# A transformer block kernel: weight remainders on GpSimd beside attentions, crossed halves of k in three stages, and another order of ScalarE's work for the queries to the memory

## The chip, the cores and the metric

The kernel runs on one core of one Trainium2 chip. The metric is the device time of one execution in microseconds (us), as the median of several runs. Five engines work side by side, each with its own queue, and wait for each other on semaphores: PE (TensorE, the matrix engine), DVE (VectorE), ACT (ScalarE), POOL (GpSimd) and SP (SyncE, which here only issues DMAs).

## The reference, cut to what matters

256 tokens of width 1024 pass through two layers of a first block (SwiGLU, a mixer, SwiGLU, a per-layer gate `ple`) and then a second block. All is in float32. The parts around the change:

```python
def swiglu(x, w_gate_up, w_down):
    g, u = jnp.split(x @ w_gate_up, 2, axis=-1)
    return (jax.nn.silu(g) * u) @ w_down

def odd_mixer(h, w_in, b_f, w_out):          # layer 1; layer 0 has two attentions (sliding window, and low-rank k and v)
    q, k, v, f_logit = jnp.split(h @ w_in, [w, 2 * w, 3 * w], axis=-1)
    logf = jax.nn.log_sigmoid(f_logit + b_f)
    out = fox_attention(q, k, v, jnp.cumsum(logf, axis=1))
    return out @ w_out

# second block
y_a = moba_attention(q, k, v) @ moba_w_proj
y_b = gmlp_spatial_gating(gu, gv, ...) @ gmlp_w_proj
x = x + (sigmoid(gate_a) * y_a + sigmoid(gate_b) * y_b) @ w_out
x = x + memory_cross_attention(rmsnorm(x, g_xa), rmsnorm(mem, g_mem), w_q, w_kv, w_o)
x = x + peer_ffn(rmsnorm(x, g_ffn), peer_w_q, subkeys, w_down, w_up)
```

## The kernel before, in words

**Weights as a stream.** All large weights are stored as 340 units of 128x2048 float32 (1 MB), four blocks of 128 rows of k by 512 columns. They pass through a ring of three buffers (`RING = 3`), the splitting two units ahead of use (`LEAD = 2`). The units by stage, first unit in brackets: `ffa0` (0), `ev_in` (33), `uq`, `ukv` (39, 40), `ev_out` (41), `ffb0` (45), `ple0` (78), `ffa1` (83), `od_in` (116), `od_out` (128), `ffb1` (132), `ple1` (165), `in2` (170), `moba` (188), `gmlp` (190), `xkv` (192), `out2` (196), `xq` (200), `xo` (202), `peer_q` (204), `peer` (212).

**Each unit, step by step.** SP loads `raw` (`load_unit`, L248); the load of unit u+3 waits until the remainder of unit u is made. ScalarE rounds it to the matrix engine's format, `w_hi` (`split_hi`, L257, one instruction, L262). VectorE makes the remainder `w_lo = raw - w_hi` (`split_lo`, L264, one instruction, L267). PE then multiplies three times into a PSUM bank: `w_hi` by `x_hi` (L300), `w_lo` by `x_hi` (L301), `w_hi` by `x_lo` (L302); a unit is 24 such matmuls of 128x512 where both token tiles use it. `take` (L293) waits for both halves of a unit before the first of them. The activations are split in the same way: ScalarE makes `x_hi` out of PSUM (L327), VectorE `x_lo` (L336), PE transposes them first (L305).

```python
def take(pe, u):
    pe.wait_ge(*act_done["w_hi", u])
    pe.wait_ge(*dve_done["w_lo", u])
    return u % RING
```

**Norms.** ScalarE sums squares (L408), VectorE takes the mean (L413), GpSimd the power -1/2 (`pool_root`, L418). Beside these GpSimd clears a few buffers (L1255 to L1257, L1478, L1832) and issues a few DMAs.

**Attentions.** A chain of steps. In each, PE makes scores (L880), VectorE the maxima (L962, L1000) and the inverse of the sums, ScalarE the exponentials (L938), VectorE scales them, two halves at a time, both operand and result in SBUF (L987, in the queries to the memory L1010), PE transposes (L305) and multiplies with the values (L907). Between the steps PE works on products of the weight units at hand, and each engine's list has the splits of the next units put in by hand.

**Order.** Every engine's program is written out by hand, in the order in which the functions `tensor_...`, `scalar_...`, `vector_...`, `pool_...` and `sync_...` call things; there is no scheduler. In a stage's first block of 512 columns the units come as k 0 to 3, then k 4 to 7 of the same block, and the second needs the second four chunks of `x_hi` and `x_lo`. In `od_in` the forget gate's small work stands between units: PE transposes its logits `zt` after unit 2, and uses their logarithm in the matmuls of L1329 after unit 3; in between VectorE and ScalarE compute it (ScalarE with two table loads, L1386 and L1388). In `scalar_cross` (L1928) the order is: squares, wait for the power (in `scalar_normed`, L428), `w_hi` of unit 202, the table load for Exp (L1933), the scaled queries (L816, `scale_out`), `w_hi` of unit 203. PE needs these queries for its transposes (L305).

Of the kernel before, what the change touches and what calls it, by code (L numbers as in the profile page):

```python
# [15 lines left out]
P = 128  # L16
# [20 lines left out]
RING = 3  # L37
# [103 lines left out]
def build(nc, a, stop=None):  # L141
    with ExitStack() as ctx:
# [121 lines left out]
        def split_lo(e, u):  # L264
            if u < N_UNITS and u not in plain:
                e.wait_ge(*act_done["w_hi", u])
                e.tensor_tensor(w_lo[:, u % RING, :, :], raw[:, u % RING, :, :], f32(w_hi[:, u % RING, :, :]),  # L267
                                ALU.subtract).then_inc(*dve_done.mark("w_lo", u))
# [24 lines left out]
        def take(pe, u):  # L293
            pe.wait_ge(*act_done["w_hi", u])
            pe.wait_ge(*dve_done["w_lo", u])
            return u % RING
# [131 lines left out]
        def scalar_normed(act, key, part, name, prev, banks=(6, 7, 2, 3)):  # L428
            for i in (0, 1):
                scalar_lift(act, key, 4 * part + 2 * i, KC, banks[2 * part + i], lambda k: gain(name, k), x_hi)  # L430
            if part:
                wait_h(act, prev, 1)
                scalar_squares(act, key, h_tile, D, 0)
                act.wait_ge(*pool_done["rstd", key])
# [8 lines left out]


# [103 lines left out]
        def tensor_up(pe, key, c, u, between=None, ready=None, meanwhile=None, free=None):  # L548
            for i in range(2):
                s = u + i if u + i < 2 else take(pe, u + i)  # L550
                for t in range(NT):
                    if i == 0 and free:
                        free(t)
                    if i == 0 and t == 1 and between:
                        between()
                    for k in range(UB):
                        kk = i * UB + k
                        if ready and t == 0:
                            ready(kk)
                        last = product(pe, bank[gu(c)[t]][:, :], s, k, BLK, x_hi[:, kk, t * P:(t + 1) * P],  # L560
                                       x_lo[:, kk, t * P:(t + 1) * P], kk == 0, kk == KC - 1)
                    last.then_inc(*pe_done.mark("unit", u + i, t))
                    if i == 1:
                        pe_done.also("up", key, c, t)
                pe_done.also("used", u + i)
                if i == 0 and meanwhile:
                    meanwhile()
# [25 lines left out]
        def tensor_ffn(pe, n, prev, hand):  # L593
# [3 lines left out]
            tensor_up(pe, n, 0, ffn_up(n, 0), lambda: tensor_normed(pe, n, prev, 1), ready)  # L597
            for c in range(1, NFC):
                def free(t, c=c):
                    pe.wait_ge(*dve_done["mid", n, 0 if c == 2 else c - 1, t])  # L600
                tensor_up(pe, n, c, ffn_up(n, c), free=free if c > 1 else None, meanwhile=lambda c=c: tensor_back(pe, n, c - 1))
                if c >= 2:
                    take_down(pe, n, c - 2)
                    for half in range(2):
                        tensor_down_half(pe, n, c - 2, half)
                    pe_done.also("used", ffn_down(n, c - 2))
# [11 lines left out]
        def scalar_ffn(act, n, prev, hand):  # L618
# [17 lines left out]
            split_hi(act, ffn_up(n, 0) + 1 + LEAD)  # L636
            silu(0)
            for c in range(1, NFC):
                split_hi(act, ffn_up(n, c) + LEAD)
                split_hi(act, ffn_up(n, c) + 1 + LEAD)  # L640
# [9 lines left out]
        def vector_ffn(dve, n, prev, hand):  # L650
# [21 lines left out]
            split_lo(dve, ffn_up(n, 0) + 1 + LEAD)  # L672
            both(0)
            for c in range(1, NFC):
                split_lo(dve, ffn_up(n, c) + LEAD)
                split_lo(dve, ffn_up(n, c) + 1 + LEAD)
# [2049 lines left out]
```

## Time and profile before

| | |
|---|---|
| runs | 2117.62 us median of 3 (2116.42 to 2120.5) |
| profiled execution, its own time | 2120.12 us |
| its span | 2118.3 us |
| granted TensorE clock, mean over it | 0.997 |
| PE busy | 99% of the span, 10466 matmuls |
| VectorE, ScalarE, GpSimd busy | 63%, 50%, 1% |
| one `w_hi` on ScalarE, one `w_lo` on VectorE | 1915 ns, 2290 ns, 336 of each |
| chain that ended last | 94% on PE |

The span runs from the first to the last instruction of the profiled execution, and its own time has 1.8 us more around it. In a timeline row the first number is the start in us from the span's beginning, the second the duration; a group of consecutive instructions of one kind has one row, with their count behind an x. The bracket at the end says how long the engine was idle before it, and what it had waited for. PEclk is the granted clock of TensorE, 1.00 for 2.4 GHz and 0.50 for 1.2 GHz.

### The profile page before, as it was taken

Reading aid. Unit: us, or ns where it says so; the run is one execution under the profiler, and the core shown is the slowest. Engines: PE = TensorE matmul, PEld = TensorE weight load, DVE = VectorE, ACT = ScalarE, POOL = GpSimd, SP = SyncE. Lnnn points to the kernel's source line nnn. Section 1 sums busy time; section 2 is a strip of 40 time slices with the busy share of each in tenths; the row PEclk is TensorE's granted clock in tenths of the full one; section 3 lists DMA queues with packets and bytes.
Section 4 is the critical chain, followed back from the end, with each engine's and each line's share of the span. In section 5 each row is a group of like instructions: output and inputs, shape, how many; then the busy total and the mean of one; then the engine's idle time right before and its main releaser. Section 6 shows DMA issues by size and latency. Waiting matters only on the chain.

```text
span 2118.3 us, 25812 instructions
## 1 busy us (share of the span) xinstructions
PE 2091.8 (99%) x10466; PEld 1744.0 (82%) x10466; DVE 1338.4 (63%) x1793; ACT 1049.0 (50%) x1262; POOL 31.2 (1%) x42
## 2 busy tenths in 40 slices
PE   9999899999999999999999999999999999999998
PEld 7888788888888888888888878888888888888887
DVE  5445765456545566554675756799888656666665
ACT  5445564446444556444657555546455544444443
POOL 0100000000000000000100000000000000000000
PEclk9999999999999999999999999999999999999999
DMA  6654335554555442555554535577799997676772
GB/s 254 215 183 177 119 133 192 196 180 180 182 196 180 177 140 105 194 183 192 186 185 160 177 119 199 179 243 238 240 270 272 281 329 310 261 268 258 268 258 109
DMA packets 96596, 433.72 MB, mean 205 GB/s; under 512 B 7680, under 2 KB 41104, under 8 KB 51936
## 3 DMA queue, kind: packets, MB, share of 16 engines
q1 hardware_dynamic: 95152, 426.50, 57.2%
q0 software_dynamic: 1328, 5.58, 0.8%
q8 instruction: 84, 1.38, 0.2%
q14 instruction: 32, 0.26, 0.0%
HBM read 397.45 MB, written 34.60 MB: 204 GB/s over the span
## 4 chain that ended last, share of the span: by engine, by line
PE 94%; DVE 3%; ACT 1%; issue 1%; DMA 0%; POOL 0%; SPq 0%; POOLq 0%; DVEq 0%
PE bank L300 28%; PE bank L302 28%; PE bank L301 28%; PE bank L305 5%; PE bank L2224 2%; DVE w_lo L267 1%; PE bank L907 1%; PE bank L880 1%; PE bank L2057 0%; DMA h<-in_x 0%; DVE x_lo L336 0%; DVE arena L800 0%; ACT w_hi L262 0%; ACT arena L938 0%; ACT x_hi L327 0%
## 5 line engine op out<-in xcount | busy, mean ns | idle before, releaser
L267 DVE TENSOR_TENSOR w_lo<-raw,w_hi 128x2048 fp32r<-128x2048 f32 x336 | 768.7, 2290 | 510.0 <-ACT w_hi L262 509.9
L262 ACT ACTIVATE w_hi<-raw 128x2048 fp32r<-128x2048 f32 x336 | 643.0, 1915 | 721.2 <-PE bank L302 704.7
L300 PE MATMUL bank<-w_hi,x_hi 128*128 128x512 f32 (+1 forms) x2080 | 822.0, 395 | 4.6 <-DVE x_lo L336 3.3
L302 PE MATMUL bank<-w_hi,x_lo 128*128 128x512 f32 (+1 forms) x2080 | 810.1, 389 | 0.0
L301 PE MATMUL bank<-w_lo,x_hi 128*128 128x512 f32 (+1 forms) x2080 | 809.4, 389 | 0.0
L300 PEld LDWEIGHTS bank<-w_hi,x_hi 128*128 128x128 f32 x2080 | 391.5, 188 | 84.0 <-ACT gated L408 3.1
L302 PEld LDWEIGHTS bank<-w_hi,x_lo 128*128 128x128 f32 x2080 | 391.0, 188 | 82.1
L301 PEld LDWEIGHTS bank<-w_lo,x_hi 128*128 128x128 f32 x2080 | 391.7, 188 | 76.2
L300 PE MATMUL bank<-w_hi,a_hi 128*128 128x512 f32 x624 | 246.6, 395 | 0.2 <-DVE a_lo L995 0.2
L302 PE MATMUL bank<-w_hi,a_lo 128*128 128x512 f32 x624 | 243.2, 390 | 0.0
L301 PE MATMUL bank<-w_lo,a_hi 128*128 128x512 f32 x624 | 243.0, 389 | 0.0
L302 PEld LDWEIGHTS bank<-w_hi,a_lo 128*128 128x128 f32 x624 | 117.1, 188 | 24.6
L300 PEld LDWEIGHTS bank<-w_hi,a_hi 128*128 128x128 f32 x624 | 117.3, 188 | 23.2 <-DVE a_lo L995 0.4
L301 PEld LDWEIGHTS bank<-w_lo,a_hi 128*128 128x128 f32 x624 | 117.3, 188 | 22.9
L622 ACT ACTIVATE gated<-bank,small 128x256 f32<-128x256 f32 x88 | 41.8, 475 | 119.6 <-PE bank L302 119.4
L2308 DVE TENSOR_TENSOR gated<-bank,arena 128x512 f32<-128x512 f32 x64 | 65.2, 1060 | 53.7 <-PE bank L305 53.7
L305 PE MATMUL bank<-consts_sb,arena 128*128 128x128 f32 (+2 forms) x566 | 78.8, 277 | 9.4 <-DVE arena L987 4.9
L305 PEld LDWEIGHTS bank<-consts_sb,arena 128*128 128x128 f32 (+2 forms) x566 | 66.5, 139 | 21.2 <-issue 4.5
L656 DVE SCALAR_TENSOR_TENSOR mid<-bank,small,gated 128x256 f32<-128x256 f32 x88 | 41.9, 479 | 44.8 <-ACT gated L622 44.8
L327 ACT ACTIVATE x_hi<-bank,gains_sb 128x256 fp32r<-128x256 f32 x92 | 36.1, 476 | 57.6 <-PE bank L305 57.6
L2214 DVE TENSOR_TENSOR arena<-arena 128x1024 bf16<-128x1024 bf16 x96 | 60.4, 683 | 0.0
L336 DVE SCALAR_TENSOR_TENSOR x_lo<-bank,gains_sb,x_hi 128x256 fp32r<-128x256 f32 x92 | 38.1, 477 | 20.7 <-ACT x_hi L327 20.5
(202 smaller groups left out, 1222.8 us busy)
## 6 DMA issues: line engine op xcount, KB each, us to landing
raw<-in_w SPq DMA_DIRECT2D x338, 1024.0 KB, 4.8
parked_t<-arena SPq DMA_DIRECT2D x32, 512.0 KB, 8.9
arena<-parked_t SPq DMA_DIRECT2D x8, 2048.0 KB, 9.4
arena<-parked_a SPq DMA_DIRECT2D x32, 512.0 KB, 5.8
parked_a<-one_i SPq DMA_DIRECT2D x21, 512.0 KB, 7.3
parked_a<-mid SPq DMA_DIRECT2D x11, 512.0 KB, 7.0
raw<-in_w SPq DMA_DIRECT2D x8, 256.0 KB, 6.3
one_i<-in_alibi POOLq DMA_DIRECT2D x1, 1024.0 KB, 5.2
```

Of the source, the lines that this page charges most:

```text
L262: act.activation(w_hi[:, u % RING, :, :], raw[:, u % RING, :, :], ACT.Copy).then_inc(*act_done.mark("w_hi", u))
L267: e.tensor_tensor(w_lo[:, u % RING, :, :], raw[:, u % RING, :, :], f32(w_hi[:, u % RING, :, :]), ALU.subtract).then_inc(*dve_done.mark("w_ ...
L300: pe.matmul(out, hi, w_hi[:, s, b, 0:width], start=start, stop=False)
L301: pe.matmul(out, hi, w_lo[:, s, b, 0:width], start=False, stop=False)
L302: return pe.matmul(out, lo, w_hi[:, s, b, 0:width], start=False, stop=stop)
L305: return pe.transpose(out, src, ident[0:src.shape[0], 0:src.shape[0]])
L336: dve.scalar_tensor_tensor(lo[:, k, :], part, gain_of(k), f32(hi[:, k, :]), ALU.mult, ALU.subtract).then_inc(*dve_done.mark("lift_lo", key ...
L622: act.activation(gated[:, 2 * (c % 2) + t, :], bank[gu(c)[t]][:, 0:FC], ACT.Silu, scale=rstd(t)).then_inc(*act_done.mark("silu", n, c, t))
L656: dve.scalar_tensor_tensor(mid[:, t, c % 2 * FC:(c % 2 + 1) * FC], bank[gu(c)[t]][:, FC:2 * FC], rstd(t), gated[:, 2 * (c % 2) + t, :], AL ...
L2214: last = dve.tensor_tensor(hot_j[:, slot, 1 + k, :, :, :], hot_j[:, slot, 0, :, :, :], token_cols(2 + k), ALU.mult)
L2224: last = pe.matmul(bank[banks[j // 4]][:, j % 4 * P:(j % 4 + 1) * P], hot_i[:, slot, j // 2, :, j % 2], hot_j[:, slot, 1 + k, j // 2, :, j ...
L2308: dve.tensor_tensor(gated[:, 2 * b:2 * b + 2, :], bank[back_banks(c)[b]][:, :].rearrange("p (f t) -> p f t", f=2), tables[:, piece % N_TAB ...
```

## The change

Three parts.

- **Remainders on GpSimd.** For the units in `lent` GpSimd makes `w_lo` instead of VectorE: units 41, 42, 43 (`ev_out`), 128, 129, 130 (`od_out`), 188, 189 (`moba`), 190, 191 (`gmlp`), 200, 201 (`xq`), 202, 203 (`xo`), 204, 205 (`peer_q`). The list holds sixteen units, and the built program has sixteen such instructions on GpSimd. The loads and PE wait for GpSimd's semaphore at those units. GpSimd's list is put in order around its powers and DMAs, and the load of `p` for `ple` moves ahead of the power of `ffb`.
- **Crossed halves.** In `ffa1`, `od_in` and `in2` the second and the third unit change places in the stored weights and in PE's order: k 0 to 3 of block 0, k 0 to 3 of block 1, k 4 to 7 of block 0, k 4 to 7 of block 1. The first block is therefore finished one unit later. In `od_in` the forget gate's logits keep their place in PE's list by count of units. Some splits move ahead of the work on block 0's result.
- **ScalarE's order in `scalar_cross`.** The Exp table load moves between the squares and the wait for the power, and `w_hi` of unit 202 moves behind the scaled queries.

```diff
+        CROSSED = ("ffa1", "od_in", "in2")
+        for n in CROSSED:
+            u = first[n]
+            stored[u + 1], stored[u + 2] = u + 2, u + 1
...
+        lent = {first[n] + i for n, units in (("ev_out", (0, 1, 2)), ("od_out", (0, 1, 2)), ("moba", (0, 1)), ("gmlp", (0, 1)),
+                                              ("xq", (0, 1)), ("xo", (0, 1)), ("peer_q", (0, 1))) for i in units}
+
+        def remainder_made(u):
+            return (pool_done if u in lent else dve_done)["w_lo", u]
...
-                sp.wait_ge(*dve_done["w_lo", u - RING])
+                sp.wait_ge(*remainder_made(u - RING))
...
+        def remainders(pool, u0, u1):
+
+            for u in range(u0, u1):
+                if u in lent:
+                    pool.wait_ge(*act_done["w_hi", u])
+                    pool.tensor_tensor(w_lo[:, u % RING, :, :], raw[:, u % RING, :, :], f32(w_hi[:, u % RING, :, :]),
+                                       ALU.subtract).then_inc(*pool_done.mark("w_lo", u))
...
+            tensor_up_half(pe, n, 0, 0, first[n], lambda: tensor_normed(pe, n, prev, 1), ready)
+            if n in CROSSED:
+                tensor_up_half(pe, n, 1, 0, first[n] + 1)
+                tensor_up_half(pe, n, 0, 1, first[n] + 2, None, ready)
+                tensor_up_half(pe, n, 1, 1, first[n] + 3)
+                tensor_back(pe, n, 0)
...
             unit(0)
+            unit(2)
             unit(1)
             pe.wait_ge(*act_done["f_hi"])
...
-            unit(2)
+            unit(3)
             pe.wait_ge(*dve_done["forget", "zt"])
...
-            unit(3)
+            unit(4)
             pe.wait_ge(*dve_done["forget", "logf"])
...
-            unit(4)
             unit(5)
...
-            for i in range(8):
+            for i in (0, 2, 1, 3, 4, 5, 6, 7):
                 unit(i)
...
-            scalar_normed(act, "xa", 1, "xa", prev, XA_BANKS)
-            split_hi(act, q0 + LEAD)
-
-            act.activation(small[:, 80:81], gains[:, 0:1], ACT.Exp, scale=0.0)
+
+            scalar_normed(act, "xa", 1, "xa", prev, XA_BANKS,
+                          lambda: act.activation(small[:, 80:81], gains[:, 0:1], ACT.Exp, scale=0.0))
             act.wait_ge(*pe_done["block", "xq", 0, 0])
             scale_out(act, 0, bank[4][:, :], qn_x[:, 0, :]).then_inc(*act_done.mark("xq"))
+            split_hi(act, q0 + LEAD)
             split_hi(act, q0 + 1 + LEAD)
```

**ScalarE, the queries to the memory.** Before (x_hi is the lift of the second token tile, gated holds the squares, L816 is the scaled queries, L938 the exponentials):

```order
L327 ACTIVATE x_hi<-bank,gains_sb 128x256 x4
L408 ACTIVATE gated,small<-h 128x1024 x2
L262 ACTIVATE w_hi<-raw 128x2048
L1933 ACT_TABLE_LOAD
L1933 ACTIVATE small<-gains_sb 128x1
L816 ACTIVATE arena<-bank,small 128x512
L262 ACTIVATE w_hi<-raw 128x2048
L938 ACTIVATE arena,stat<-bank,stat 128x256 x4
```

and now:

```order
L348 ACTIVATE x_hi<-bank,gains_sb 128x256 x4
L429 ACTIVATE gated,small<-h 128x1024 x2
L1977 ACT_TABLE_LOAD
L1977 ACTIVATE small<-gains_sb 128x1
L857 ACTIVATE arena<-bank,small 128x512
L275 ACTIVATE w_hi<-raw 128x2048 x2
L979 ACTIVATE arena,stat<-bank,stat 128x256 x4
```

The table load stands right behind the squares, and both weight splits stand behind the scaled queries.

**VectorE, at the start of the even attentions** (L800 and L817 take projected queries out of PSUM, L1014 and L1015 begin the rotation). Before:

```order
L800 TENSOR_SCALAR arena<-bank 64x256 x4
L267 TENSOR_TENSOR w_lo<-raw,w_hi 128x2048
L817 TENSOR_SCALAR arena<-bank,small 128x384
L1014 TENSOR_TENSOR arena<-arena,consts_sb 128x256
L1015 TENSOR_TENSOR arena<-arena,consts_sb 128x256
```

and now:

```order
L841 TENSOR_SCALAR arena<-bank 64x256 x4
L858 TENSOR_SCALAR arena<-bank,small 128x384
L1055 TENSOR_TENSOR arena<-arena,consts_sb 128x256
L1056 TENSOR_TENSOR arena<-arena,consts_sb 128x256
```

The remainder of unit 41 is gone from VectorE. It stands on GpSimd, as one of the three in the second row here (the rows around it are powers and the load of `p`):

```order
L439 TENSOR_TENSOR small<-small,consts_sb 128x2 x3
L288 TENSOR_TENSOR w_lo<-raw,w_hi 128x2048 x3
L820 DMA arena<-in_p 128x512
L439 TENSOR_TENSOR small<-small,consts_sb 128x2 x3
```

GpSimd had no remainder at all before.

**VectorE, the forget gate in `od_in`** (L1426 to L1436 take the logits to their logarithm, L817 is the first block's result). Before:

```order
L267 TENSOR_TENSOR w_lo<-raw,w_hi 128x2048
L817 TENSOR_SCALAR arena<-bank,small 128x8x64
L1421 COPY one_i<-bank 16x256
L267 TENSOR_TENSOR w_lo<-raw,w_hi 128x2048
L1426 SCALAR_TENSOR_TENSOR one_i<-bank,small,one_i 128x16 x2
L1429 TENSOR_SCALAR one_i<-one_i 128x32
L1431 TENSOR_TENSOR one_i<-one_i 128x32
L1433 TENSOR_SCALAR one_i<-one_i 128x32
L1436 TENSOR_TENSOR one_i<-one_i 128x32
L267 TENSOR_TENSOR w_lo<-raw,w_hi 128x2048
```

and now:

```order
L280 TENSOR_TENSOR w_lo<-raw,w_hi 128x2048 x2
L858 TENSOR_SCALAR arena<-bank,small 128x8x64
L1463 COPY one_i<-bank 16x256
L1467 SCALAR_TENSOR_TENSOR one_i<-bank,small,one_i 128x16 x2
L1470 TENSOR_SCALAR one_i<-one_i 128x32
L1472 TENSOR_TENSOR one_i<-one_i 128x32
L1474 TENSOR_SCALAR one_i<-one_i 128x32
L1477 TENSOR_TENSOR one_i<-one_i 128x32
L280 TENSOR_TENSOR w_lo<-raw,w_hi 128x2048
```

Two remainders stand ahead of the first block's result, and the next one still stands behind the gate's chain.

## Rows read from the trace of the kernel before

**Rows 1.** The page's busy times: busy us, share of the span, instructions.
```profile
PE 2091.8 (99%) x10466; PEld 1744.0 (82%) x10466; DVE 1338.4 (63%) x1793; ACT 1049.0 (50%) x1262; POOL 31.2 (1%) x42
```

**Rows 2.** The waits of PE, whole span: total us, times, longest.
```profile
PE bank L305 <- DVE arena L987: 4.9, 5, 1.9
PE bank L300 <- DVE x_lo L336: 3.3, 4, 1.2
...
PE bank L305 <- ACT arena L816: 2.6, 1, 2.6
```

**Rows 3.** Busy time by window: us, busy (x instructions) per engine, PEclk, DMA share, GB/s.
```profile
245.50:252.20 6.70, 5.91 (x25) 5.19 (x24) 4.70 (x21) 3.13 (x14) 0.00 (x0) 0.50 0.07 29
...
1255.90:1259.10 3.20, 3.01 (x9) 2.56 (x10) 1.13 (x2) 1.94 (x2) 0.00 (x0) 0.50 0.47 141
```

**Rows 4.** Timeline (start us, us, engine line op, idle before), VectorE and PE, start of ffa1.
```profile
520.41 4.49 DVE L267 TENSOR_TENSOR w_lo<-raw,w_hi 128x2048 fp32r<-128x2048 f32 x2
524.82 1.65 DVE L336 SCALAR_TENSOR_TENSOR x_lo<-bank,gains_sb,x_hi 128x256 fp32r<-128x256 f32 x4
...
525.83 0.47 PE L300 MATMUL bank<-w_hi,x_hi 128*128 128x512 f32 x1 [1.18 <-DVE x_lo L336]
```

**Rows 5.** Timeline, PE at the start of in2.
```profile
1058.75 0.47 PE L300 MATMUL bank<-w_hi,x_hi 128*128 128x512 f32 x1 [1.18 <-DVE x_lo L336]
```

**Rows 6.** Timeline, od_in after the forget gate's transposes.
```profile
727.05 0.29 PE L305 MATMUL bank<-consts_sb,one_i 16*128 16x16 f32 x2
...
731.85 2.29 DVE L267 TENSOR_TENSOR w_lo<-raw,w_hi 128x2048 fp32r<-128x2048 f32 x1 [1.55 <-ACT w_hi L262]
...
732.86 0.74 PE L1329 MATMUL bank<-one_i,consts_sb 128*128 128x16 f32 x6
...
733.45 0.49 PE L300 MATMUL bank<-w_hi,x_hi 128*128 128x512 f32 x1
```

**Rows 7.** Timeline, start of the two even attentions (ev_out).
```profile
234.31 2.29 DVE L267 TENSOR_TENSOR w_lo<-raw,w_hi 128x2048 fp32r<-128x2048 f32 x1
...
237.35 1.95 PE L460 MATMUL bank<-raw,mid 128*128 128x512 f32 x4 [0.54 <-ACT arena L816]
...
241.66 0.60 PE L880 MATMUL bank<-arena 128*128 128x128 f32 x3 [0.59 <-DVE one_j L959]
```

**Rows 8.** Timeline, the even attentions at the remainder of unit 42.
```profile
268.22 2.28 DVE L267 TENSOR_TENSOR w_lo<-raw,w_hi 128x2048 fp32r<-128x2048 f32 x1
...
272.04 0.41 PE L305 MATMUL bank<-consts_sb,arena 128*128 128x128 f32 x2 [0.98 <-DVE arena L987]
```

**Rows 9.** Timeline, end of the moba attentions and gMLP.
```profile
1183.32 0.87 PE L305 MATMUL bank<-consts_sb,arena 128*128 128x128 f32 x6 [0.61 <-DVE arena L1794]
```

**Rows 10.** Timeline, queries to the memory, ScalarE and PE.
```profile
1252.03 1.92 ACT L262 ACTIVATE w_hi<-raw 128x2048 fp32r<-128x2048 f32 x1 [1.00 <-POOL small L418]
1253.96 1.28 ACT L1933 ACT_TABLE_LOAD   x1
...
1256.09 0.69 PE L305 MATMUL bank<-consts_sb,arena 128*128 128x128 f32 x2 [2.59 <-ACT arena L816]
...
1263.11 1.10 PE L305 MATMUL bank<-consts_sb,arena 128*128 128x128 f32 x6 [0.43 <-DVE arena L1010]
```

**Rows 11.** Timeline, GpSimd clears a buffer while VectorE makes a remainder.
```profile
528.38 3.56 POOL L1478 MEMSET arena<- 128x4096 f32 x1
...
529.38 2.29 DVE L267 TENSOR_TENSOR w_lo<-raw,w_hi 128x2048 fp32r<-128x2048 f32 x1 [2.83 <-ACT w_hi L262]
```

**Rows 12.** Groups of VectorE by shape: count, busy us, mean ns, idle before.
```profile
L987 DVE TENSOR_SCALAR arena<-arena,stat 128x256 f32<-128x256 f32 x24 | 7.4, 350 | 0.3
...
L987 DVE TENSOR_SCALAR arena<-arena,stat 128x128 f32<-128x128 f32 x24 | 5.8, 284 | 0.3
```

**Rows 13.** Timeline, the first unit of the queries: its w_hi, and PE's first product.
```profile
1231.49 1.92 ACT L262 ACTIVATE w_hi<-raw 128x2048 fp32r<-128x2048 f32 x1 [3.52 <-PE bank L302]
...
1238.34 0.48 PE L300 MATMUL bank<-w_hi,x_hi 128*128 128x512 f32 x1
```

More of the change, by code:

```diff
@@ L546, in ffn_down, with tensor_up_half @@
             return first[n] + (3 * c + 6 if c < NFC - 2 else 2 * NFC + c)
[L548 to L567, printed above, removed]
+        def tensor_up_half(pe, key, c, i, u, between=None, ready=None, free=None):
+            s = u if u < 2 else take(pe, u)
+            for t in range(NT):
+                if free:
+                    free(t)
+                if t == 1 and between:
+                    between()
+                for k in range(UB):
+                    kk = i * UB + k
+                    if ready and t == 0:
+                        ready(kk)
+                    last = product(pe, bank[gu(c)[t]][:, :], s, k, BLK, x_hi[:, kk, t * P:(t + 1) * P],
+                                   x_lo[:, kk, t * P:(t + 1) * P], kk == 0, kk == KC - 1)
+                last.then_inc(*pe_done.mark("unit", u, t))
+                if i == 1:
+                    pe_done.also("up", key, c, t)
+            pe_done.also("used", u)
         def tensor_down_half(pe, key, c, half):
@@ L671, in vector_ffn @@
                 vector_first_rest(dve)
-            split_lo(dve, ffn_up(n, 0) + 1 + LEAD)
-            both(0)
+            split_lo(dve, first[n] + 1 + LEAD)
+            if n not in CROSSED:
+                both(0)
             for c in range(1, NFC):
                 split_lo(dve, ffn_up(n, c) + LEAD)
+                if n in CROSSED and c == 1:
+                    both(0)
                 split_lo(dve, ffn_up(n, c) + 1 + LEAD)
@@ L1833, in pool_moba @@
             pool.memset(values_m, 0.0).then_inc(*pool_done.mark("cleared", "moba"))
+            remainders(pool, first["ple_gate1"] + LEAD, first["in2"] + LEAD)
             pool_root(pool, "final1", 40)
             pool_root(pool, "mix2", 0)
+            remainders(pool, first["in2"] + LEAD, first["moba"] + LEAD)
             pool.wait_ge(*dve_done["o_lo", "M", 7])
@@ L1838, in pool_moba @@
             pool_root(pool, "v", 24)
+            remainders(pool, first["moba"] + LEAD, first["gmlp"] + LEAD)
             pool_root(pool, "mem", 32)
+            remainders(pool, first["gmlp"] + LEAD, first["xq"] + LEAD)
         kt_x, qn_x, qt_x = view(2048, HEADS_X, T), view(4096, NT, 512), view(5120, HEADS_X, T)
@@ L2454, in pool_peer @@
             pool.dma_start(keys, a["subkeys"]).then_inc(keys_loaded, 16)
+            remainders(pool, first["xo"] + LEAD, q0 + LEAD + 1)
             pool_root(pool, "ffn", 0)
+            remainders(pool, q0 + LEAD + 1, q0 + UPS + LEAD + 6)
             for i in (1, 2):
@@ L2458, in pool_peer @@
             pool.dma_start(final_row, a["final_g"].partition_broadcast(P)).then_inc(final_g_loaded, 16)
+            remainders(pool, q0 + UPS + LEAD + 6, N_UNITS)
         def sync_peer(sp):
```

90 lines of the change are left out of this document (59 added, 31 removed).

## The prediction

> **What bounds the kernel now.** I read the page's busy times first: PE is busy for 99% of the span [rows 1]. A change can therefore win only where PE stands still or runs slowly, and lose only where it makes PE stand still. The waits of PE name these places [rows 2]: L987, the scaling inside the attentions, 4.9 us in five waits; `x_lo` (L336), 3.3 us in four; the scaled queries to the memory (L816), one wait of 2.6 us. The windows show the other loss [rows 3]: in two stretches, of 6.7 and of 3.2 us, the granted clock is 0.50, which is the 1.2 GHz level. Both follow work with gaps. Everything else is matmuls that the change leaves as they are. The pool to win from is thus some 15 us of 2118. The sum is made against the profiled execution, 2120.1 us; the median of the runs is 2.5 us lower, and the difference is applied to it. This kernel's measurement can tell about 0.2%, 4.2 us, from no change.
>
> **Crossed halves.** In `ffa1` VectorE makes two remainders (520.41 to 524.90) ahead of the second half of `x_lo`, and PE waits 1.18 us for it [rows 4]. With the crossing PE has one more unit (24 matmuls) that needs only the first four chunks, and 24 matmuls are 5.6 us by the stretch from 727.28 to 732.86 [rows 6]. That covers the wait: -1.2. `in2` has the same row with the same 1.18 [rows 5]: -1.2. In both, the result of block 0 is lifted a unit later, which PE's next need of it (the bank of block 2, two blocks on) hides by a unit; without that cover each would give back what it is late.
>
> In `od_in` the `x_lo` wait is one of the two left in the sum (3.3 - 2.4 = 0.9, [rows 2]), so -0.5. But the forget gate gives it back. Today PE does two units between the transposes of its logits (727.05) and the use of the unit whose remainder starts at 731.85 and ends at 734.14, because `w_hi` of that unit stands behind ScalarE's gate with two table loads. Afterwards only one unit and the L1329 matmuls (732.86 to 733.45) lie between: PE is ready at 733.45 and waits until 734.14 [rows 6]: +0.7. Net +0.2.
>
> **Remainders on GpSimd: the price.** No row shows a subtraction of this size on GpSimd. A clear of 128x4096 takes 3.56 us [rows 11], so one pass over 2048 columns is 1.8 us. The remainder reads two streams and writes one. From below it is 2.3 us, VectorE's own time for it [rows 11]; from above three passes in a row, 5.3 us. I take 4.4, between two and three passes, since GpSimd's write pass alone comes near VectorE's whole instruction. GpSimd is idle otherwise (31 us of work, [rows 1]), so sixteen of these, 70 us, only matter where someone waits for one of them.
>
> The Trainium skill, *GPSIMD Engine Reference*, section 3.1, states 4497 ns for this shape on GpSimd and 2293 ns on VectorE. VectorE's figure agrees with the 2.29 us here; no row shows GpSimd's. By it the sum would come out as it does.
>
> Where is there room? Unit 200: `w_hi` ends at 1233.41 and PE's first product is at 1238.34 [rows 13], 4.9 us: covered at 4.4, and 0.4 us of waiting at 5.3. It is the shortest of the sixteen; I count it and the others at nothing. The loads of the next units wait 2 us longer for such a remainder, and have whole attentions (tens of us) as cover.
>
> **What VectorE gains.** At the start of the even attentions the remainder of unit 41 (234.31, 2.29 us) stands ahead of the queries that PE waits for twice, 0.54 and 0.59 us [rows 7]. Both go: -1.1. The stretch at half clock just behind it I leave as it is. The remainder of unit 42 (268.22, 2.28 us) delays a score step, and PE waits 0.98 for the L987 behind it [rows 8]: -1.0. At the end of moba PE waits 0.61 for L1794, behind two remainders [rows 9]: -0.5. `peer_q` and the rest: -0.1. Together -2.7.
>
> **ScalarE's order.** Today ScalarE idles 1.00 us for the power, then does `w_hi` (1252.03, 1.92 us), the table load (1.28) and only then the queries; PE waits 2.59 us [rows 10]. Afterwards the table load starts at 1251.03 beside GpSimd's power and ends at 1252.3; the queries (0.7 us) are done by 1253.1, before PE is through with its products at 1253.5. The wait goes: -2.6. `w_hi` of unit 202 ends some 1.3 us later than now and that of unit 203 earlier; with GpSimd both remainders are ready by 1264, and PE uses them after the attention. The half clock of 3.2 us follows this wait [rows 3] and goes with it. PE was busy for 3.0 us of it, worth half: -1.5. From below this term is 0. Together -4.1.
>
> **The sum.** -1.2 - 1.2 + 0.2 - 2.7 - 4.1 = -9.0 us: 2111.1 for a profiled execution, 2108.6 for the median.
>
> **Rival A: VectorE and GpSimd get in each other's way.** L987 takes 284 ns for 128 columns and 350 ns for 256 [rows 12], 0.52 ns for each further column, while a remainder has 2.29 us for 2048, 1.12 ns each [rows 11]. So the scaling from SBUF to SBUF runs at double rate, and uses twice the width for it. If GpSimd's remainder needs part of that width, a scaling (L987, L1010) that comes due while it runs waits for its end; so may VectorE's own operations with two operands in SBUF. Then the remainder of unit 42, which GpSimd can start half a microsecond before VectorE does now (267.7), runs to 272.1 in place of 270.5, and the L987 behind it comes 0.7 us later than now, not 1.0 earlier; two of them end to end hold off the last operations of moba in the same way, +0.7 instead of -0.5; `peer_q` costs 0.5. In the queries `w_hi` of 202 would end at 1255.0, so that 202 and 203 run back to back on GpSimd until 1263.9, while L1010 is due 2.6 us before its place of now, at about 1260. PE's L305 behind it would come at 1264.6 in place of 1263.11 [rows 10]: +1.5 instead of -4.1. The crossings and the start of the even attentions stay: -2.4 + 0.2 - 1.1 + 0.7 + 0.7 + 0.5 + 1.5 = +0.1, a median of 2118. What speaks for it is the double rate; what speaks against it is that a VectorE remainder at 529.38 kept its 2.29 us under a GpSimd clear [rows 11], but that clear reads nothing.
>
> The Trainium skill, *SBUF — State Buffer*, section "Who interferes with whom", states this rule: the port pair that both engines share is an exclusive lock, held for the whole instruction by whoever issues first, and it concerns VectorE's double-rate operations and those with two inputs in SBUF. The undisturbed remainder under the clear agrees with its exception for a GpSimd instruction that only writes; no row here tests the rest.
>
> **Rival B: slower.** The same, at a remainder of 5.3 us, with the pairs of scalings split: one half gets in between two remainders, the other waits for the second. 202 and 203 end at 1265.7, so +3.3 in the queries, and PE idles there for some 6 us, behind which the clock stays low for another stretch like the one of now [rows 3], +1.5; unit 42 costs +1.6, by the 0.9 us of its remainder's length, and unit 200 +0.4: -3.3 + 3.3 + 1.5 + 1.6 + 0.7 + 0.5 + 0.4 = +4.7, a median of 2122.3. It decides from a remainder of some 5 us together with the lock.
>
> **Rival C: the first half clock goes too.** If attentions that start 1.1 us earlier keep the clock up at 245.5 [rows 3], about 2 us more come back, since most of that stretch waits for VectorE and ScalarE and not for PE: 2106.6.
>
> **How the numbers follow.** Forecast 0.46, rival A 0.34, rival B 0.13, rival C 0.07. The range from 2105.5 to 2120.5 holds the forecast with its price bounds, A and C but not B, and leaves out some 0.18 in all. The forecast's own range is 2106 to 2113: the clock's 1.5 and 2 us of waits may stay. Faster by over 0.2% (under 2113.4): the forecast and C less 0.03, 0.50. Within 0.2%: A and a little of the forecast, 0.37. Slower: 0.13.
>
> **What would show it.** Right: no wait for `x_lo` at the start of `ffa1` and `in2`; a wait of about 0.7 us in `od_in` behind the L1329 matmuls; GpSimd's remainders at about 4.4 us; no wait for the scaled queries near 1253, and clock 1.0 behind it; L987 and L1010 at their means of 284 and 350 ns. Wrong: an L987 or L1010 that takes microseconds, or starts with the end of a GpSimd remainder; PE waiting for a GpSimd remainder at all; a new stretch at 0.50.

## The result, and the profile after

| | before | changed |
|---|---|---|
| runs | 2117.19 us median of 6 (2116.42 to 2120.50) | 2124.86 us median of 6 (2124.28 to 2125.51) |
| profiled execution, its span | 2120.12, 2118.3 us | 2124.49, 2122.6 us |
| GpSimd busy | 31.2 us | 104.6 us |

The changed kernel is slower: ratio 1.0034, 95% interval 1.0023 to 1.0045, 7.7 us by the medians. The two profiled executions are only 4.4 us apart, since that of before happens to lie 2.9 us over its median and that of the changed kernel 0.4 under its own.

The waits of PE over the whole span, which answer to [rows 2] (L326 is the former L305, L1028 the former L987, L1051 the former L1010, L357 the former L336, L1835 the former L1794):

```profile
PE bank L326 <- DVE arena L1028: 7.8, 6, 3.7
PE bank L326 <- DVE arena L1051: 5.8, 1, 5.8
...
PE bank L326 <- DVE arena L1835: 2.1, 1, 2.1
PE bank L321 <- DVE x_lo L357: 2.1, 2, 1.7
```

What was to go has gone: the wait for the scaled queries (2.6 us) is no longer in the list, and of the four waits for `x_lo` two remain, one of them a new one of 1.7 us. What has come is on VectorE: L1028 has 7.8 us instead of 4.9, L1051 5.8 instead of 0.4, L1835 2.1 instead of 0.6. No wait for a `w_lo` is in the list, so PE never stood for a GpSimd remainder itself.

The groups of VectorE by shape (count, busy us, mean ns, idle before) answer to [rows 12]; the next row is GpSimd's remainder on the page:

```profile
L1028 DVE TENSOR_SCALAR arena<-arena,stat 128x128 f32<-128x128 f32 x24 | 10.0, 461 | 0.3
L1051 DVE TENSOR_SCALAR arena<-arena,stat 128x256 f32<-128x256 f32 x8 | 7.9, 1024 | 0.1
L1028 DVE TENSOR_SCALAR arena<-arena,stat 128x256 f32<-128x256 f32 x24 | 7.4, 351 | 0.3
```
```profile
L288 POOL TENSOR_TENSOR w_lo<-raw,w_hi 128x2048 fp32r<-128x2048 f32 x16 | 73.4, 4598 | 296.0 <-ACT w_hi L275 296.0
```

A mean that rises while the shape stays is the mark of something held: the same 128x128 scaling that took 284 ns on average takes 461, and the scalings of the queries to the memory 1024 instead of 350. The timelines show which ones. First the even attentions, VectorE and then GpSimd and PE (the row of VectorE at 264.15 holds the two halves of one scaling; the first takes 0.29 us, and the second has the row at 264.36):

```profile
264.15 4.74 DVE L1028 TENSOR_SCALAR arena<-arena,stat 128x128 f32<-128x128 f32 x2
...
264.36 4.53 DVE L1028 TENSOR_SCALAR arena<-arena,stat 128x128 f32<-128x128 f32 x1
268.81 0.28 DVE L1036 TENSOR_TENSOR a_lo<-bank,a_hi 128x128 fp32r<-128x128 f32 x1
```
```profile
264.30 4.51 POOL L288 TENSOR_TENSOR w_lo<-raw,w_hi 128x2048 fp32r<-128x2048 f32 x1 [29.53 <-ACT w_hi L275]
```
```profile
269.04 0.45 PE L326 MATMUL bank<-consts_sb,arena 128*128 128x128 f32 x1 [3.67 <-DVE arena L1028]
```

GpSimd's remainder of unit 42 starts at 264.30, between the starts of the two halves (264.15 and 264.36), and the second half ends with it, at 268.89 against 268.81. Next the queries to the memory, the same three engines:

```profile
1258.39 1.51 DVE L1051 TENSOR_SCALAR arena<-arena,stat 128x256 f32<-128x256 f32 x1
...
1258.39 6.01 DVE L1051 TENSOR_SCALAR arena<-arena,stat 128x256 f32<-128x256 f32 x2
1264.33 0.74 DVE L858 TENSOR_SCALAR arena<-bank,small 128x512 f32<-128x512 f32 x1
```
```profile
1255.18 9.07 POOL L288 TENSOR_TENSOR w_lo<-raw,w_hi 128x2048 fp32r<-128x2048 f32 x2 [3.00 <-ACT w_hi L275]
```
```profile
1264.46 0.47 PE L326 MATMUL bank<-consts_sb,arena 128*128 128x128 f32 x1 [5.84 <-DVE arena L1051]
```

The first row of VectorE is the first half alone: it was issued under unit 202's remainder and ended at 1259.90, where that one ends (1259.75). The second half then waited for unit 203's remainder, until 1264.40. The other two held operations have two operands in SBUF, gMLP's L1840 (0.69 us in the kernel before) and VectorE's own remainder of unit 206 (2.29 us):

```profile
1179.17 0.69 DVE L1835 TENSOR_TENSOR arena<-bank,gains_sb 128x512 f32<-128x512 f32 x1 [1.04 <-PE bank L1634]
1179.89 2.92 DVE L1840 TENSOR_TENSOR arena<-arena 128x512 f32<-128x512 f32 x1
...
1288.44 5.00 DVE L280 TENSOR_TENSOR w_lo<-raw,w_hi 128x2048 fp32r<-128x2048 f32 x1 [1.32 <-ACT w_hi L275]
```
```profile
1172.75 9.51 POOL L288 TENSOR_TENSOR w_lo<-raw,w_hi 128x2048 fp32r<-128x2048 f32 x2 [0.88 <-ACT w_hi L275]
...
1286.68 4.61 POOL L288 TENSOR_TENSOR w_lo<-raw,w_hi 128x2048 fp32r<-128x2048 f32 x1 [2.87 <-ACT w_hi L275]
```

GpSimd's rows are the remainders of units 190 and 191 (the second from 1177.76 to 1182.26) and that of 205 (until 1291.29). L1840 ends 0.55 us after its one, VectorE's remainder of 206 ends 2.15 us after its one: each has nearly its own length left when GpSimd is done.

L1835, right before L1840, has one operand in PSUM and one in SBUF, lies under the same GpSimd remainder and keeps its 0.69 us.

**The account.** The same instruction of PE starts at these times in the two profiled executions; each difference less the one before it is what the stretch between won or lost.

| place | before | changed | difference | the stretch |
|---|---|---|---|---|
| even attentions, second scores | 241.66 | 239.27 | -2.4 | -0.9 at the program's start (not the change's), -1.5 by unit 41 |
| behind the stretch at half clock | 253.25 | 250.03 | -3.2 | -0.8, the stretch is shorter (not shown to be the change's) |
| behind unit 42 | 272.04 | 273.33 | +1.3 | +4.5: the wait of 3.7, and the clock behind it |
| `ffa1`, fifth chunk | 525.83 | 526.20 | +0.4 | +0.4 of clock behind unit 42, -1.3 by the crossing |
| `od_in`, fifth chunk | 713.14 | 712.73 | -0.4 | -0.8 |
| `od_in`, unit 121 | 739.03 | 739.20 | +0.2 | +0.6, the wait for `w_hi` |
| `in2`, fifth chunk | 1058.75 | 1057.74 | -1.0 | -1.2 |
| end of moba and gMLP | 1183.32 | 1183.47 | +0.2 | +1.2, L1840 |
| queries, transposes | 1256.09 | 1253.52 | -2.6 | -2.7, ScalarE's order |
| queries, first scaling used | 1263.11 | 1264.46 | +1.3 | +3.9, L1051 |
| `peer_q` | 1290.54 | 1294.38 | +3.8 | +0.8 of clock, +1.6 by the remainder of 206 |

Two rows are differences between executions and no effect that can be shown. Up to 13 us into the program both kernels do the same, and there one execution is 0.9 us ahead. The stretch at half clock of the even attentions lasts 6.8 us in the kernel before and 3.4 us here, but two runs of one and the same kernel (e8_early and e10_again, below) also have 3.4 and 6.8 us there.

The clock, in windows over the two long waits (columns as in [rows 3]):

```profile
267.00:275.00 8.00, 5.96 (x22) 5.14 (x23) 4.96 (x12) 1.87 (x8) 1.81 (x1) 0.57 0.37 131
1260.00:1268.00 8.00, 3.54 (x15) 3.25 (x16) 5.75 (x5) 1.54 (x3) 4.25 (x1) 0.57 0.69 244
```

A mean of 0.57 over 8 us is 6.8 us at 0.50 and the rest at 1.00. The first did not exist before. The second stands in place of the one at 1255.9: the waits removed there came back behind it.

### The profile page after: what moved, and what is told of

It is laid out like the page before. It is cut to its first block, busy times and chain, and to the rows that moved or that the text cites. A ratio compares the mean times of both kernels' runs of the same rounds, so it can differ in the third digit from the quotient of the medians.

```text
span 2122.6 us, 25813 instructions
## 1 busy us (share of the span) xinstructions
PE 2090.3 (98%) x10466; PEld 1745.1 (82%) x10466; DVE 1318.3 (62%) x1777; ACT 1048.3 (49%) x1262; POOL 104.6 (5%) x58
## 4 chain that ended last, share of the span: by engine, by line
PE 95%; DVE 2%; ACT 1%; issue 1%; DMA 0%; SPq 0%; POOLq 0%; POOL 0%; DVEq 0%; ACTq 0%
PE bank L321 29%; PE bank L323 28%; PE bank L322 28%; PE bank L326 5%; PE bank L2269 2%; PE bank L948 1%; PE bank L921 1%; DVE w_lo L280 0%; ACT w_hi L275 0%; PE bank L2102 0%; DVE arena L1028 0%; DVE arena L1051 0%; PE bank L487 0%; DMA h<-in_x 0%; ACT arena L979 0%
## 5 line engine op out<-in xcount | busy, mean ns | idle before, releaser
L280 DVE TENSOR_TENSOR w_lo<-raw,w_hi 128x2048 fp32r<-128x2048 f32 x320 | 735.0, 2299 | 490.4 <-ACT w_hi L275 490.3
L326 PE MATMUL bank<-consts_sb,arena 128*128 128x128 f32 (+2 forms) x566 | 79.1, 279 | 16.5 <-DVE arena L1028 7.8
L326 PEld LDWEIGHTS bank<-consts_sb,arena 128*128 128x128 f32 (+2 forms) x566 | 67.3, 139 | 27.5 <-issue 7.4
L288 POOL TENSOR_TENSOR w_lo<-raw,w_hi 128x2048 fp32r<-128x2048 f32 x16 | 73.4, 4598 | 296.0 <-ACT w_hi L275 296.0
```

The costliest lines, as they stand in the source:

```text
L280: dve.tensor_tensor(w_lo[:, u % RING, :, :], raw[:, u % RING, :, :], f32(w_hi[:, u % RING, :, :]), ALU.subtract).then_inc(*dve_done.mark(" ...
L288: pool.tensor_tensor(w_lo[:, u % RING, :, :], raw[:, u % RING, :, :], f32(w_hi[:, u % RING, :, :]), ALU.subtract).then_inc(*pool_done.mark ...
L326: return pe.transpose(out, src, ident[0:src.shape[0], 0:src.shape[0]])
```

## The experiments

Two theories stood at the start. **Held:** the loss comes only from VectorE operations at double rate, or with both operands in SBUF, that stand still while GpSimd makes a remainder; the rest of the change wins what it was costed at. **Rival:** one of the other two parts, or the sheer length of GpSimd's remainders and the later loads behind them, is a loss too.

### One part at a time

Four kernels, each the changed kernel with parts taken back.

```diff
 # e1_crossing: only the crossed halves
+        lent = set()
 # and scalar_cross, vector_cross in the old order
 # e2_lending: only the sixteen remainders on GpSimd
+        CROSSED = ()
 # and the old order of the units in od_in and in2, of scalar_cross and vector_cross
 # e3_order: only ScalarE's order in scalar_cross
+        lent = set()
+        CROSSED = ()
 # e4_without: two crossings, ScalarE's order, one remainder on GpSimd
+        lent = {first["ev_out"]}
+        CROSSED = ("ffa1", "in2")
```

One thing goes with ScalarE's order that the description of the change doesn't name: `split_lo` of unit 202 moves two scalings later in VectorE's list (`vector_cross`). In the changed kernel GpSimd makes this remainder and the move has no effect; in e3_order VectorE makes it, so that e3_order tests both moves together.

> Only the crossed halves in ffa1, od_in and in2; all remainders on VectorE, ScalarE's order for the queries to the memory as before. Theory (the loss comes only from VectorE operations held by GpSimd remainders): the crossings keep what the changed kernel's trace shows for them, 1.2 us each in ffa1 and in2, 0.2 in od_in (0.8 won, 0.6 lost at the unit behind the forget gate), so 2 to 3 us faster than before. Rival (the crossings lose somewhere that is hidden in the changed kernel's sum): no change or slower than before.

> Only the sixteen remainders on GpSimd; no crossing, ScalarE's old order. Theory: unit 41 wins 1.5 to 2.3 us, unit 42 costs 4.9, units 190 and 191 1.2, unit 205 1.6; in the queries to the memory GpSimd's second remainder runs from 1258.5 to 1263.1 and the scaling is due at 1262.45, so only 0.7 is lost there: 4 to 7 us slower than before, 2121 to 2124. Rival (the queries to the memory are slow because of ScalarE's new order, and GpSimd costs little): within 2 us of before.

> Only ScalarE's order for the queries to the memory (with VectorE's remainder of unit 202 two scalings later, as in the changed kernel); all remainders on VectorE, no crossing. Theory: PE's wait of 2.6 us for the scaled queries goes and the clock stays up, with nothing on GpSimd that could hold the scaling: 3 to 4.5 us faster than before. Rival (the new order is itself the loss, by the later w_hi of unit 202): slower than before by 1 us or more.

> Crossings in ffa1 and in2 but not od_in, ScalarE's new order, and GpSimd makes one remainder only, unit 41, under which VectorE does nothing but move PSUM to SBUF. Theory: the parts add, 1.3 + 1.3 + 4 + 1.5 to 2.3: 8 to 9 us faster than before, some 2108.5. Rival (the gains overlap in the clock's stretches, and the clock falls elsewhere): 5 us faster or less.

| kernel | median | ratio to before, 95% interval |
|---|---|---|
| before | 2117.33 (21 runs) | |
| e1_crossing | 2114.07 | 0.9987 (0.9978 to 0.9996) |
| e2_lending | 2126.92 | 1.0043 (1.0030 to 1.0057) |
| e3_order | 2113.37 | 0.9981 (0.9972 to 0.9990) |
| e4_without | 2110.14 | 0.9964 (0.9950 to 0.9977) |

The crossings win 3.3 us (2 to 3 expected) and ScalarE's order 4.0 (3 to 4.5 expected), and the rival that either is a loss falls. In e3_order's trace the same PE instructions gain 2.7 us where the wait for the scaled queries was and 1.5 us in the stretch that ran at half clock behind it. e4_without is 7.2 us faster, a little less than the 8 to 9 expected and more than the 5 of its rival. The remainders on GpSimd alone lose 9.6 us, more than the 4 to 7 I expected. The three parts add up to -3.3 - 4.0 + 9.6 = +2.3, while together they give +7.7: ScalarE's order, worth 4.0 with all remainders on VectorE, brings the first scaling ahead to where it lies under a GpSimd remainder. In e2_lending, with the old order, only one half of it is caught, and for less:

```profile
1264.06 2.47 DVE L1051 TENSOR_SCALAR arena<-arena,stat 128x256 f32<-128x256 f32 x2
1266.44 0.74 DVE L858 TENSOR_SCALAR arena<-bank,small 128x512 f32<-128x512 f32 x1
```

The pair takes 2.47 us instead of 0.61, a loss of 1.9, against 5.4 in the changed kernel (6.01 less 0.61). What e2_lending lost beyond my 4 to 7 us is in its own windows: behind the wait of 2.1 us at gMLP its clock fell, where the changed kernel, with the same wait at the same place, kept its own. The window of e2_lending and then that of the changed kernel:

```profile
1183.00:1190.00 7.00, 6.23 (x21) 5.46 (x22) 4.94 (x12) 5.01 (x11) 0.04 (x1) 0.51 0.44 150
```
```profile
1183.00:1190.00 7.00, 6.45 (x34) 5.38 (x35) 4.51 (x11) 5.80 (x11) 0.69 (x1) 1.00 0.44 150
```

21 matmuls against 34 in 7 us; by the starts of the same PE instructions e2_lending fell 2.6 us further behind there. What decides whether the clock falls behind a wait of this length stays open.

The same comparison, PE instruction by PE instruction between e2_lending and the changed kernel, gives the price of ScalarE's order beside the remainders on GpSimd. Behind gMLP (1190.77 in e2_lending, 1187.92 in the changed kernel) the changed kernel is 2.85 us ahead, behind the first scalings of the queries (1273.77 and 1271.22) 2.55. So the order, worth 4.0 us alone, costs 0.3 us here. The rest of the difference of 2.5 us between the two profiled executions lies elsewhere: the crossings put the changed kernel 2.8 us ahead and the clock behind gMLP 2.7, but behind unit 42 it stood 2.7 us back (270.66 against 273.33), although the two programs are the same up to there: 1.3 us at the program's start, and the rest in the clock. The medians add up only with such differences, so that the 5.4 us by which the whole loses more than its parts is only in its larger part, some 4.3 us, shown to be the order's.

### Is it the held operations, or the length of GpSimd's remainders?

```diff
 # e5_unheld: the changed kernel, with the six remainders under which PE's operations were held back on VectorE
+        lent = {first[n] + i for n, units in (("ev_out", (0, 2)), ("od_out", (0, 1, 2)), ("moba", (0, 1)), ("xq", (0, 1)), ("peer_q", (0,))) for i in units}
```

> The changed kernel with ten of its sixteen remainders on GpSimd: 41, 43, 128, 129, 130, 188, 189, 200, 201, 204. The six under which a VectorE operation that PE waits for stood still (42, 190, 191, 202, 203, 205) are back on VectorE. Theory (a GpSimd remainder costs only by the VectorE operations that it holds): the parts of the change add up without its loss, the crossings' 3.3, the order's 4.0 and 0 to 2 for unit 41: 7 to 9 us faster than before, 2108 to 2110.5, although ten remainders still take 4.6 us each. Rival (the length of the GpSimd remainders, or the later loads behind them, costs by itself): 2113 or more.

Measured: 2109.89 us, ratio 0.9963 (0.9949 to 0.9976), 7.3 us faster than before. That is within the 7 to 9 us of the theory. Ten GpSimd remainders remain, of 4518 to 4612 ns each, and cost nothing that can be measured. Every VectorE operation that comes due under them reads PSUM, but for two scalings with their reciprocals (units 128 and 129), of which one half each takes 0.54 to 0.55 us instead of 0.35. The view of GpSimd's remainders in this kernel (duration ns min/median/max) and the two kinds of scalings:

```profile
L287 POOL TENSOR_TENSOR w_lo<-raw,w_hi x10: 4518/4582/4612, 230.4 to 1266.9; 128x2048 fp32r<-128x2048 f32 x10
```
```profile
L1027 DVE TENSOR_SCALAR arena<-arena,stat 128x128 f32<-128x128 f32 x24 | 5.8, 283 | 0.3
...
L1050 DVE TENSOR_SCALAR arena<-arena,stat 128x256 f32<-128x256 f32 x8 | 2.5, 351 | 0.1
```

The means are those of [rows 12] again. The rival (length or loads) falls for these ten; for the two in the queries to the memory it is tested next, and for the other four it rests on the changed kernel's list of waits, where PE waits for held operations and never for a `w_lo`.

### The same remainders, but the scaling on ScalarE

```diff
 # e6_scaling: the changed kernel; scaling of steps 0 and 1 of the queries to the memory on ScalarE
+                if r < 2:
+                    return
...
+            def scalar_scale(self, act, r):
+                key, m = self.key, len(self.keys(self.steps[r][0])) * P
+                act.wait_ge(*dve_done["inverse", key, r])
+                for j in range(2):
+                    cols = self.ex_at(r)[:, j * m:(j + 1) * m]
+                    last = act.activation(cols, cols, ACT.Copy, scale=self.col(4, r)[:, j:j + 1])
+                last.then_inc(*act_done.mark("scaled", key, r))
...
+            att_x.scalar_scale(act, 0)
+            att_x.scalar_scale(act, 1)
```

> The changed kernel, with the scalings of steps 0 and 1 of the queries to the memory made by ScalarE (activation with the inverse as scale) instead of VectorE's double-rate L1051; GpSimd's remainders of 202 and 203 stay where they are. Theory (the scaling waits for the port that GpSimd holds, and ScalarE has its own): these scalings take 0.4 us each right behind the exponentials, PE's wait of 5.8 us at 1264 shrinks to under 1.5 us and the clock stays up behind it: 4 to 7 us faster than the changed kernel, 2118 to 2121. Rival (the wait there comes from something else that GpSimd's remainders delay, such as w_lo or a load): within 1 us of the changed kernel's 2124.9.

Measured: 2119.07 us (11 runs), ratio to before 1.0007 (0.9998 to 1.0016), so 5.8 us below the changed kernel. GpSimd's two remainders have their old place and length (they start 1.0 us later, as everything there does), and four scalings run under them on ScalarE in 1.70 us. GpSimd, ScalarE and PE:

```profile
1256.21 9.04 POOL L288 TENSOR_TENSOR w_lo<-raw,w_hi 128x2048 fp32r<-128x2048 f32 x2 [3.00 <-ACT w_hi L275]
```
```profile
1259.94 1.70 ACT L1061 ACTIVATE arena<-arena,stat 128x256 f32<-128x256 f32 x4
```
```profile
1260.90 0.33 PE L326 MATMUL bank<-consts_sb,arena 128*128 128x128 f32 x1 [1.30 <-ACT arena L1061]
```

PE's wait of 5.84 us is 1.30, and the stretch at half clock behind it is gone:

```profile
1260.00:1268.00 8.00, 6.65 (x44) 5.91 (x45) 4.07 (x14) 6.46 (x21) 5.25 (x2) 1.00 0.56 190
```

By the same PE instructions this stage won 5.5 us. Nothing was changed in the remainders, their place or their length, so the wait was for the scaling on VectorE and nothing else behind GpSimd.

### Which kinds of instruction exclude each other

```diff
 # e7_clear: the kernel before, with three write-only GpSimd instructions from the end of w_hi of unit 42
+            pool.wait_ge(*act_done["w_hi", spare - 1])
+            for i in range(3):
+                pool.memset(f32(w_lo[:, spare % RING, :, :]), 0.0).then_inc(*pool_done.mark("cleared", "spare"))
+                pool.wait_ge(*pool_done["cleared", "spare"])
```

(`spare` is the slot of unit 43, which nothing uses at that time.)

> The kernel before, with three GpSimd clears of 128x2048 (1.84 us each, write only, into a buffer that nothing reads there) started at the end of w_hi of unit 42, in the middle of VectorE's double-rate scalings L987 and its remainder of unit 42. It tells which of GpSimd's ports matter. Theory (both engines need the write port too when VectorE runs at double rate): a scaling L987 that comes due under a clear is held until its end, up to 1.8 us instead of 0.28, while the remainder with two operands in SBUF keeps its 2.29 us. Rival (only GpSimd's reads hold VectorE): all scalings stay at 0.28.

VectorE, with L989 the scaling and L269 the remainder of unit 42, and GpSimd:

```profile
265.80 1.91 DVE L989 TENSOR_SCALAR arena<-arena,stat 128x128 f32<-128x128 f32 x1
266.00 1.72 DVE L997 TENSOR_TENSOR a_lo<-bank,a_hi 128x128 fp32r<-128x128 f32 x1
266.20 2.28 DVE L269 TENSOR_TENSOR w_lo<-raw,w_hi 128x2048 fp32r<-128x2048 f32 x1
...
269.39 2.11 DVE L989 TENSOR_SCALAR arena<-arena,stat 128x128 f32<-128x128 f32 x2
```
```profile
265.79 5.63 POOL L2602 MEMSET w_lo<- 128x2048 f32 x3 [46.41 <-PE bank L909]
```

The scaling that came due under a clear took 1.91 us instead of 0.28 and ended with the clear (1.84 us from 265.79); so did the second half of the next pair. The remainder with two operands in SBUF kept its 2.28 us although nearly all of it lay under clears. So GpSimd's write alone holds an operation at double rate, and a clear doesn't hold one with two operands, which a remainder on GpSimd, reading as well, did hold. The hold is of another kind here. The remainder stands behind the held scaling in VectorE's queue, and yet its row starts at 266.20 and ends at 268.48, only 0.77 us after the scaling: VectorE went on while the scaling waited for its end. Under GpSimd's remainder of unit 42 the next instruction (L1036) had to wait until 268.81. L997, between the two, ends with the scaling (1.72 us instead of 0.28), and PE waited 1.05 us for it; how VectorE keeps the three apart no run here shows. One execution of this kernel took 2119.91 us, within what before takes.

### A version without the loss

```diff
 # e8_early: all three crossings, ScalarE's order, unit 41 on GpSimd; the split of unit 121 ahead of the forget gate's chain
+        lent = {first["ev_out"]}
...
             out_c(act, 0, 0)
+            split_hi(act, o0 + 3 + LEAD)
             act.wait_ge(*dve_done["forget", "below"])
...
-            split_hi(act, o0 + 3 + LEAD)
             out_c(act, 0, 1)
...
+            split_lo(dve, o0 + 3 + LEAD)
             dve.wait_ge(*pe_done["forget", 1])
...
-            split_lo(dve, o0 + 3 + LEAD)
             out_c(dve, 1, 1)
 # e9_none: the same, no remainder on GpSimd
+        lent = set()
 # e11_190: the same as e8_early, unit 190 on GpSimd too
+        lent = {first["ev_out"], first["gmlp"]}
```

> All three crossings, ScalarE's new order, only unit 41 on GpSimd; and in od_in both halves of the split of unit 121 stand ahead of the forget gate's chain instead of behind it. Theory (PE's new wait of 0.7 us in od_in is for w_hi of unit 121 behind the two table loads): that wait goes, so 0.8 us beyond the crossings of ffa1 and in2, the order and unit 41: about 0.8 to 1.4 us faster than the kernel with two crossings (2110.1), so 2108.5 to 2109.5. Rival (the early split collides with the first block's lift): no faster than 2110.

> The kernel of e8_early without any remainder on GpSimd (unit 41 back on VectorE). Theory (unit 41 on GpSimd frees VectorE ahead of the even attentions, where PE waited 0.54 and 0.59 us): 0.8 to 1.5 us slower than the kernel with unit 41 on GpSimd, about 2110.5. Rival (what starts earlier there waits later): the same as with it, 2109.5.

> The same kernel as e8_early, run beside the one without a GpSimd remainder on the same chip, so that they can be compared: 2109 to 2110 by every theory.

> e8_early with unit 190's remainder on GpSimd too, whose place (1173 to 1178 in the changed kernel) ends before the two-operand L1840 of gMLP comes due at 1180. Theory (only the operations that come due under a remainder are held, here none that PE waits for, and VectorE reaches L1835 earlier): PE's wait of 0.61 us behind moba shrinks, 0 to 0.6 us faster than e8_early. Rival (the remainder of 191 on VectorE, also with two operands in SBUF, waits for GpSimd and takes the gain back or more): the same or up to 1 us slower.

| kernel | median | ratio to before, 95% interval |
|---|---|---|
| e8_early | 2109.49 | 0.9964 (0.9950 to 0.9978) |
| e10_again, the same kernel | 2107.63 | 0.9958 (0.9944 to 0.9971) |
| e9_none | 2110.17 | 0.9964 (0.9951 to 0.9978) |
| e11_190 | 2109.10 | 0.9963 (0.9950 to 0.9977) |

All are 6.9 to 9.5 us faster than before, and the runs don't tell them apart: the same kernel gave 2109.5 and 2107.6. In e8_early PE's wait for `w_hi` in `od_in` (0.7 us in the changed kernel) is gone from its list of waits, so the early split does what it was meant to, for less than the total can show. That unit 41 or 190 on GpSimd helps could not be shown: without any remainder on GpSimd the kernel is as fast within the intervals, where I had expected it 0.8 to 1.5 us slower. For unit 190 the trace speaks for the rival of e11_190: VectorE's remainder of unit 191, due under GpSimd's of unit 190, takes 3.23 us instead of 2.29, and PE's waits for L1834 (the former L1794) grow from 0.6 to 1.6 us.

```profile
1165.35 5.05 POOL L287 TENSOR_TENSOR w_lo<-raw,w_hi 128x2048 fp32r<-128x2048 f32 x1 [0.88 <-ACT w_hi L274]
```
```profile
1169.32 3.23 DVE L279 TENSOR_TENSOR w_lo<-raw,w_hi 128x2048 fp32r<-128x2048 f32 x1 [1.32 <-ACT w_hi L274]
```

## Why the prediction was wrong

The forecast of 2108.6, the range up to 2120.5 and the chance of 0.50 for faster were wrong; the changed kernel takes 2124.9. The sum had the parts right that don't touch GpSimd, and failed at one step: it let VectorE's operations keep their lengths beside GpSimd's remainders, which was to win 2.7 us, while the remainders on GpSimd alone lose 9.6.

- **Crossed halves**, forecast -2.2 with `od_in` at +0.2: the account shows -1.3, -1.2 and -0.8 + 0.6 (so `od_in` wins 0.2 where it was to lose 0.2), and alone they gave 3.3 us (interval 0.9 to 4.7). Right, with the new wait in `od_in` of 0.68 us where 0.7 was forecast.
- **ScalarE's order**, forecast -4.1: alone 4.0, of which 1.5 in the clock's stretch as forecast. Right where nothing is on GpSimd; beside GpSimd's remainders the same gain came and was lost again at the scalings behind it. In the changed kernel the table load runs from 1251.23 and the queries are done at 1253.30, before PE's transposes at 1253.52.
- **The price of a GpSimd remainder**, 4.4 taken between 2.3 and 5.3: 4.60 in the mean, 4.51 to 4.61 but for one of 5.05. Right; unit 200 was covered. The 4497 ns of the Trainium skill (*GPSIMD Engine Reference*, section 3.1) is within 3% of the mean.
- **What VectorE gains**, forecast -2.7: this is the step that failed, and with it the end of the step on ScalarE's order. I let VectorE's operations keep their lengths beside a GpSimd remainder. Unit 41 behaved so (-1.5, since VectorE only moved PSUM to SBUF there), but unit 42 costs 3.7 us of waiting instead of saving 1.0, gMLP 2.1 instead of 0, the queries to the memory 5.8, `peer_q` 1.7.
- **Rival A** named the mechanism, and e5_unheld, e6_scaling and e7_clear show it. I gave it 0.34, although the double rate stood in [rows 12]. What I held against it was a VectorE remainder that kept its 2.29 us under a clear; e7_clear shows that such a remainder does so while a scaling is held, so it was no evidence. The rule in the Trainium skill (*SBUF — State Buffer*, "Who interferes with whom") also spoke against the change: an exclusive lock for the whole instruction, on operations at double rate, and on those with two operands in SBUF against a GpSimd instruction that reads. The runs here agree with each clause of it: 4.53 us under a remainder and 1.91 under a clear for a scaling of 0.28, 5.00 and 2.28 for VectorE's remainder.
- **Rival A's sizes** were too small because I set the two engines' times in a row and not against each other. For unit 42 I had GpSimd begin at 267.7 and let the loss be the later end, 0.7 us; in fact it fell between the starts of the halves of a pair, and the second half stood for the whole of it. The trace of before has such a pair right there (`267.62 0.48 DVE L987 TENSOR_SCALAR arena<-arena,stat 128x128 f32<-128x128 f32 x2`). For the remainder of 206 I counted 0.5 and it was 1.6. Only the queries came as it says: the first scaling used is 1.2 us later (forecast +1.5), with 0.8 us of clock behind it that A doesn't have.
- **Rival B**, 2122.3, is the nearest to the outcome, though still 2.6 us short of it: in the queries one half of the pair got in between the two remainders and the other waited for the second, as it says. That its sum comes near is luck in part: it has 4.8 us in the queries where 2.0 were lost, and 1.6 at unit 42 where 4.9 were lost, clock included. Its threshold was wrong: I let it decide only from a remainder of some 5 us, and 4.6 was enough, since it needs only that a pair comes due while two remainders run end to end.
- **Rival C** is open: the first stretch at half clock was 3.4 us instead of 6.8, but its length differs as much between runs of one kernel.

The parts together are worse than their sum: ScalarE's order brought the queries 2.7 us ahead, the scaling behind them into the two remainders, and so took back its own gain.

## What to carry to other kernels

Before a piece of work goes to an idle engine, list what the engine it leaves will be doing at that time, and look for operations at twice the usual rate (a second shape of the same line gives the rate) and for those with all operands in SBUF: beside a GpSimd instruction that reads and writes SBUF they don't slow down, they stop until it has ended. What is left of GpSimd's time is then paid in full by whoever waits for them, and on the path that PE waits for the price is up to GpSimd's length, not the shorter one it replaces. So lend only under operations that read PSUM; here that did no harm (ten lent units in e5_unheld), and no run shows that it gained anything. Two short operations in a row are the worst case: the second is caught by the next long one.

## What the runs showed of the hardware that I had not expected

- A VectorE scaling of 0.28 us took 4.53 us under one GpSimd instruction of 4.51 us, and a scaling pair was split by a GpSimd instruction that started in the 0.2 us between the starts of its halves.
- It goes both ways: unit 190's remainder began at 1172.75, while VectorE's L1815 with two operands in SBUF still ran until 1173.32, and took 5.05 us where the others took 4.51 to 4.61. It is 5.05 us again in e2_lending, e6_scaling and e11_190.
- A GpSimd instruction that only writes holds a double-rate VectorE operation for its whole length too (1.91 us under a clear of 1.84), but VectorE goes on with a remainder meanwhile.
- PE's clock fell to half behind a wait of 2.1 us in e2_lending (0.51 over the 7 us behind it) and in e6_scaling, and not in the changed kernel with the same wait in the same place (1.00); in e2_lending this moved the time by 2.6 us.
